# Last norm by rows, squares shared by two engines, a finer weave for one S5 group and for the first key steps

## What is computed

```
x <- LN0(a*x + 0.5*SwiGLU_1(x));  x <- LN1(a*x + Mix(x));  x <- LN2(a*x + 0.5*SwiGLU_2(x))
LN(x) = (x - mean) * rsqrt(mean((x - mean)^2) + 1e-5) * gain + bias        over the 1024 features
```

## Time and profile before

| | us |
|---|---|
| median of 3 runs (2525.97 to 2529.35) | 2529.04 |
| the profiled execution, its own time | 2529.85 |
| its span in the trace | 2528.2 |
| PE busy / DVE / ACT / POOL | 2406.3 / 1628.0 / 1086.1 / 458.9 |
| mean granted clock of PE, as a share of full | 0.982 |

### The profile page before, as it was taken

How to read it: one execution, slowest core, us unless ns; L and a number is a source line. 1 busy time by engine, 2 the same in 40 slices (tenths; PEclk the granted TensorE clock), 3 DMA queues, 4 the chain that set the end, 5 groups by cost and what they waited for, 6 DMA issues and landing times.

```text
span 2528.2 us, 46326 instructions
## 1 busy us (share of the span) xinstructions
PE 2406.3 (95%) x18811; PEld 2268.4 (90%) x18811; DVE 1628.0 (64%) x2536; ACT 1086.1 (43%) x1663; POOL 458.9 (18%) x532
## 2 busy tenths in 40 slices
PE   7999999999998999999999999999999889999998
PEld 6988998999787777789999999999999889999997
DVE  4787776665764555567686566466656585587555
ACT  3433455433553333443254534554433537354333
POOL 4896800002100111200111101021001000121000
PEclk9999999999999999999899999999999999999999
DMA  8667776445346777644566556555555556555553
GB/s 179 176 177 190 205 198 192 125 117 143 116 136 207 221 239 226 164 123 128 142 175 175 164 148 208 169 153 150 154 149 148 169 165 215 156 158 146 150 150 96
DMA packets 676278, 417.31 MB, mean 165 GB/s; under 512 B 31555, under 2 KB 639683, under 8 KB 676067
## 3 DMA queue, kind: packets, MB, share of 16 engines
q1 hardware_dynamic: 669538, 393.98, 54.1%
q0 software_dynamic: 6528, 20.37, 2.5%
HBM read 395.51 MB, written 18.78 MB: 164 GB/s over the span
## 4 chain that ended last, share of the span: by engine, by line
PE 78%; DVE 12%; issue 3%; ACT 3%; DMA 2%; SPq 2%; POOL 0%; POOLq 0%; ACTq 0%; DVEq 0%
PE ps L256 21%; PE ps L257 20%; PE ps L258 20%; DVE w_lo L251 4%; PE ps L881 2%; PE ps L882 2%; PE ps L883 2%; ACT w_hi L242 2%; PE ps L2280 1%; PE ps L1593 1%; PE ps L1642 1%; DMA w_raw<-in_ffn_w_up 1%; DVE x L531 1%; PE ps L1614 1%; DVE h_lo L435 1%
## 5 line engine op out<-in xcount | busy, mean ns | idle before, releaser
L251 DVE TENSOR_TENSOR w_lo<-w_raw,w_hi 128x1024 fp32r<-128x1024 f32 (+1 forms) x648 | 825.0, 1278 | 623.9 <-ACT w_hi L242 620.9
L256 PE MATMUL ps<-x_hi,w_hi 128*128 128x256 f32 (+1 forms) x3200 | 969.3, 303 | 49.4 <-DVE w_lo L251 35.9
L257 PE MATMUL ps<-x_lo,w_hi 128*128 128x256 f32 (+1 forms) x3200 | 955.9, 299 | 0.0
L258 PE MATMUL ps<-x_hi,w_lo 128*128 128x256 f32 (+1 forms) x3200 | 955.5, 299 | 0.0
L242 ACT ACTIVATE w_hi<-w_raw 128x1024 fp32r<-128x1024 f32 (+1 forms) x648 | 669.6, 1035 | 553.8 <-PE ps L258 399.5
L256 PEld LDWEIGHTS ps<-x_hi,w_hi 128*128 128x128 f32 x3200 | 616.2, 193 | 68.4 <-DVE w_lo L251 53.6
L257 PEld LDWEIGHTS ps<-x_lo,w_hi 128*128 128x128 f32 x3200 | 616.7, 193 | 1.1 <-issue 0.2
L258 PEld LDWEIGHTS ps<-x_hi,w_lo 128*128 128x128 f32 x3200 | 616.1, 193 | 0.0
L256 PE MATMUL ps<-h_hi,w_hi 128*128 128x256 f32 (+1 forms) x1408 | 423.9, 301 | 12.3 <-DVE w_lo L251 9.5
L257 PE MATMUL ps<-h_lo,w_hi 128*128 128x256 f32 (+1 forms) x1408 | 414.5, 294 | 0.0
L258 PE MATMUL ps<-h_hi,w_lo 128*128 128x256 f32 (+1 forms) x1408 | 414.4, 294 | 0.0
(11 more groups left out here) (263 smaller groups left out, 2192.8 us busy)
## 6 DMA issues: line engine op xcount, KB each, us to landing
w_raw<-in_ffn_w_gate SPq DMA_DIRECT2D x176, 512.0 KB, 4.2
w_raw<-in_ffn_w_up SPq DMA_DIRECT2D x176, 512.0 KB, 3.9
w_raw<-in_ffn_w_down SPq DMA_DIRECT2D x128, 512.0 KB, 4.0
w_raw<-in_w_in_ab SPq DMA_DIRECT2D x56, 512.0 KB, 4.0
w_raw<-in_ffn_w_down SPq DMA_DIRECT2D x64, 384.0 KB, 3.5
arena<-in_cache_k SPq DMA_DIRECT2D x64, 256.0 KB, 4.2
arena<-in_cache_v POOLq DMA_DIRECT2D x64, 256.0 KB, 4.8
w_raw<-in_w_out_ab SPq DMA_DIRECT2D x16, 512.0 KB, 3.9
```

Of the source, the lines that this page charges most:

```text
L251: dve.tensor_tensor(T.w_lo[:, u % RING, 0:n], T.w_raw[:, u % RAW, 0:n], T.w_hi[:, u % RING, 0:n].bitcast(F32), ALU.subtract).then_inc(T.w_ ...
L256: pe.matmul(out, w_hi, m_hi, start=first, stop=False)
L257: pe.matmul(out, w_hi, m_lo, start=False, stop=False)
L258: return pe.matmul(out, w_lo, m_hi, start=False, stop=last)
```

## The change

- `LastNorm` takes the place of N5B. DVE makes eight diagonal matrices of the gain during the last FFN, and SP loads the bias along rows. At the end PE multiplies the centred x by a diagonal, which turns it to rows and scales it by the gain (`to_rows`, 12 matmuls for each half of the features); ACT squares all eight blocks into eight buffers; PE sums the squares to one column for each token (24 matmuls with one moving column); ACT takes the root of 128x2 and 64x1 values and DVE inverts them; six DVE instructions multiply by the inverse root, add the bias and write the rows. Reciprocal, scaling and bias over 128x320 fall away, and the six copies and the 24 transposes.
- N0B, N2B and N3B are `shared`: POOL adds the squares of blocks 0 to 3 only, DVE adds those of 4 to 7 in step 3, and PE sums both, with two matmuls.
- In `f3a[:2]` the FFN yields after each product (`fine`), so that a side step follows each product and not each pair. `beside_b` takes the norm, the 11 input steps and the 14 scan steps singly, with six empty places between scan steps (`stretched`), and the outputs in pairs.
- `slowly` takes steps 0 to 4 singly, then (5, 6) and (7, 8) as pairs, so that all later steps come two main steps later.

```diff
-def ffn_tensor(T, pe, Q):
+def ffn_tensor(T, pe, Q, fine):
...
                     .then_inc(T.w_used.h, 1)
+                if fine and s == 0:
+                    yield
...
-            if i == self.var_at and self.alone:
-                for k in range(KT):
-                    pe.wait_ge(T.squared.h, self.squared + k + 1)
-                    pe.matmul(self.root_of, T.ones[:, :], T.sq[:, k % 4, 0:self.g.n], start=(k == 0), stop=(k == KT - 1))\
-                      .then_inc(T.sq_added.h, 1)
+            if i == self.var_at and self.shared is not None:
+                pe.wait_ge(T.sq_added.h, self.sq_added + 3)
+                pe.wait_ge(T.sq_shared.h, self.shared + 3)
+                pe.matmul(self.ps, T.ones[:, :], self.acc2, start=True, stop=False)
+                pe.matmul(self.ps, T.ones[:, :], self.acc, start=False, stop=True).then_inc(T.var_done.h, 1)
...
+            if i == self.square_at + 2 and self.shared is not None:
+                for k in range(5, KT):
+                    dve.wait_ge(T.squared.h, self.squared + k + 1)
+                    if k > 5:
+                        dve.wait_ge(T.sq_shared.h, self.shared + k - 5)
+                    dve.tensor_tensor(self.acc, T.sq[:, 0, 0:self.g.n] if k == 5 else self.acc, T.sq[:, k % 4, 0:self.g.n],
+                                      ALU.add).then_inc(T.sq_shared.h, 1)
...
+class LastNorm(Norm):
...
+    def tensor(self, pe, moved):
+        T = self.T
+        pe.wait_ge(T.acc_added.h, self.added + KT - 1)
...
+        pe.matmul(self.ps, T.ones[:, :], self.acc, start=True, stop=True).then_inc(T.sum_done.h, 1)
+        pe.wait_ge(T.const_ready.h, 4 + KT)
+        self.to_rows(pe, 0)
+        for k in range(KT):
+            pe.wait_ge(T.squared.h, self.squared + k + 1)
+            for i, t in enumerate(self.g.tiles):
+                m = P if t < PT else NS
+                mm = pe.matmul(self.var_ps[0:m, i:i + 1], self.sq[:, k, i * P:i * P + m], T.ones[:, 0:1],
+                               start=(k == 0 and i == 0), stop=(k == KT - 1), skip_group_check=True)
+        mm.then_inc(T.var_done.h, 1)
+        self.to_rows(pe, 1)
+
+    def to_rows(self, pe, q):
+        T = self.T
+        for k in range(4 * q, 4 * q + 4):
+            pe.wait_ge(T.centred.h, self.centred + k + 1)
+            for n, (t, of, m) in enumerate(self.places):
+                if of == q:
+                    mm = pe.matmul(T.ps[0:m, self.bank(n), (k % 4) * P:(k % 4 + 1) * P], T.x[:, k, t * P:t * P + m],
+                                   self.diag[:, k, :], start=True, stop=True)
+        mm.then_inc(T.y_turned.h, 1)
...
+    def vector(self, dve, rows, turned):
...
+        T.dve_chain(dve, dve.reciprocal(self.by_row[:, 0:2], self.by_row[:, 0:2]))
+        T.dve_chain(dve, dve.reciprocal(self.by_row[0:NS, 2:3], self.by_row[0:NS, 2:3]))
...
+            dve.scalar_tensor_tensor(rows[0:m, t, cols], T.ps[0:m, self.bank(n), :], self.by_row[0:m, i:i + 1],
+                                     self.bias_rows[0:m, cols], ALU.mult, ALU.add).then_inc(T.y_moved[0].h, 1)
...
-            return paced(steps, [s for s in range(AttendSamples.STEPS) if s >= 8 and s % 8 < 4])
+            return paced(steps, [s for s in range(AttendSamples.STEPS) if s < 5 or s >= 8 and s % 8 < 4])
...
-            first = Norm.STEPS - 2
-            return paced(norm_and_s5(norm, s5), range(first, first + S5Group.INPUTS))
+            scan = Norm.STEPS - 2 + S5Group.INPUTS
+            return stretched(paced(norm_and_s5(norm, s5), range(scan + S5Group.SCAN)), range(scan, scan + 12, 2))
```

More of the change, by code:

```diff
@@ L129, in paired, with spaced, stretched @@
     yield
+def spaced(steps):
+    for _ in steps:
+        yield
+        yield
+def stretched(steps, long):
+    for i, _ in enumerate(steps):
+        yield
+        if i in long:
+            yield
 def paced(steps, alone):
@@ L451, in ffn_gpsimd @@
             Q.norm.add(pool, d, Q.res)
+        if fine and d is None:
+            yield
         yield
@@ L461, with __init__ @@
     STEPS = 9
-    def __init__(self, T, g, row, scale, products, alone=False, slack=0):
-        self.alone, self.steps, n = alone, self.STEPS + 3 * slack, slack
+    def __init__(self, T, g, row, scale, products, slack=0, shared=False):
+        self.shared = T.sq_shared.take(3) if shared else None
+        self.steps, n = self.STEPS + 3 * slack, slack
         self.square_at, self.var_at, self.root_at = 1 + n, 4 + n, 4 + 2 * n
@@ L477, in __init__ @@
         self.sq_added, self.var, self.rooted, self.normed = (
-            c.take(k) for c, k in ((T.sq_added, KT if alone else KT - 1), (T.var_done, 1), (T.rstd_ready, 2), (T.normed, KT)))
+            c.take(k) for c, k in ((T.sq_added, 3 if shared else KT - 1), (T.var_done, 1), (T.rstd_ready, 2), (T.normed, KT)))
         self.affine, self.rounded, self.ready = (
@@ L572, in gpsimd @@
         for i in range(self.steps):
-            if i in (self.square_at, self.square_at + 1) and not self.alone:
+            if i in (self.square_at, self.square_at + 1):
                 for k in self.half(i, self.square_at):
-                    if k == 0:
+                    if k == 0 or k >= 4 and self.shared is not None:
                         continue
@@ L2771, in layers, with ffn @@
         F3B = Ffn(B, ffn_3, N4B.ready, N4B.affine + KT)
-        N5B = Norm(T, B, 5, 2.0, False, alone=True)
+        N5B = LastNorm(T, M, B, 5, 2.0, TT * D_MODEL)
         f3b = parts(F3B, (0, 1, 2), N5B)
-        before = {A: 0, B: 2 * len(A.tiles)}
-        whole = {A: N5A.affine + KT, B: N5B.affine + KT}
+        turned_a = 2 * len(A.tiles)
         y_rows = cut(0, TT, D_MODEL)
         block = ctx.enter_context(nc.Block())
-        def ffn(of, eng, parts):
+        def ffn(of, eng, parts, fine=False):
             for part in parts:
-                yield from of(T, eng, part)
-        def store_columns(pe, g):
-            yield from store_tensor(T, pe, g, before[g], whole[g])
+                yield from of(T, eng, part, fine)
         def norm_and_s5(norm, s5):
@@ L2835, in _ @@
             run(ffn(ffn_sync, sp, f2b))
-            weave(ffn(ffn_sync, sp, f3a[:2]), beside_b(idle(Norm.STEPS), s5_b.sync(sp, O)))
+            weave(ffn(ffn_sync, sp, f3a[:2], True), beside_b(idle(Norm.STEPS), s5_b.sync(sp, O)))
             run(out_sync(T, sp, OB2))
+            sp.wait_ge(T.res_done.h, OB2.res + KT)
+            N5B.load(sp, I["ln_b"][DEPTH - 1, 2])
             run(ffn(ffn_sync, sp, f3a[2:]))
@@ L2913, in _ @@
             weave(ffn(ffn_vector, dve, f2b), N4A.vector(dve))
-            weave(ffn(ffn_vector, dve, f3a[:2]), beside_b(N3B.vector(dve), s5_b.vector(dve)))
+            weave(ffn(ffn_vector, dve, f3a[:2], True), beside_b(N3B.vector(dve), s5_b.vector(dve)))
             run(out_vector(T, dve, OB2))
             weave(ffn(ffn_vector, dve, f3a[2:]), N4B.vector(dve))
-            weave(ffn(ffn_vector, dve, f3b), after(N5A.vector(dve), store_vector(T, dve, A, y_rows, before[A])))
-            run(after(N5B.vector(dve), store_vector(T, dve, B, y_rows, before[B])))
+            weave(ffn(ffn_vector, dve, f3b), after(after(N5A.vector(dve), store_vector(T, dve, A, y_rows, 0)),
+                                                    N5B.diagonals(dve)))
+            N5B.vector(dve, y_rows, turned_a)
         @block.gpsimd
@@ L2943, in _ @@
             weave(ffn(ffn_gpsimd, pool, f2b), N4A.gpsimd(pool))
-            weave(ffn(ffn_gpsimd, pool, f3a[:2]), beside_b(N3B.gpsimd(pool), s5_b.gpsimd(pool)))
+            weave(ffn(ffn_gpsimd, pool, f3a[:2], True), beside_b(N3B.gpsimd(pool), s5_b.gpsimd(pool)))
             run(out_gpsimd(T, pool, OB2))
```

96 lines of the change are left out of this document (72 added, 24 removed).

## The result

The changed kernel takes 2536.23 us (median of 8 runs, 2529.37 to 2541.2), the kernel before 2528.85 beside it (8 runs, 2525.97 to 2532.47). The ratio is 1.0027, with a 95% interval of 1.0018 to 1.0035: 6.8 us slower by the ratio, where 13.4 faster was forecast. The profiled run of the changed kernel is the fastest of its eight, 2529.37 us with a span of 2527.7. Since it is 6.9 us under its own median, a second trace of the same kernel was taken later (e15, span 2536.4), and both are read here.

The account below looks back on a forecast made before the run. PE was taken as the bound (busy 2406.3 of 2528.2 us), leaving its idle and low-clock time. Terms -3.2 + 0.5 - 3.7 - 7.0 = -13.4 from 2529.85 gave 2516.4, stated as 2516; 8-in-10 range 2505 to 2529.

Parts of the forecast that it names:

- the likeliest case: Whole kernel: the forecast itself, 13.4 us less, 2516 us, own range 2509 to 2523; chance 0.56.
- The third rival: Whole kernel: slower end and fine weave with more long waits, each costing 3.4 us at low clock; 2537 us; chance 0.10.
- one-column matmuls may leave the clock low, and the end is 2.2 slower: Last norm, clause of the third rival: one-column sums may keep the clock low, end 2.2 us slower.
- three new places in S5: Group B's S5, clause of the third rival: new waits over 3 us at three places, S5 6.5 us slower.
- The end, -3.2 forecast: From the last product: row products, one-column sums and six DVE instructions replace the old chain; 3.2 us less.
- 2.2 more: Upper bound of the end's term: 2.2 us more if the clock is low throughout.
- Shared norms, +0.5 forecast: N0B and N2B: DVE's adds finish earlier, but PE pays one more matmul; 0.5 us more, bounds 1 less, 2 more.
- Group B's S5, -3.7 forecast: N3B and S5: 1.8 us more at norm and transposes, scan 6.6 less, 1.1 given back; 3.7 us less.
- 18.5 lost: Group B's scan before the change: 58.8 us for 14 products worth 40.3 us, so 18.5 us lost.
- Key steps, -7.0 forecast: First key steps: single steps shorten PE's waits and avoid a clock fall; 7.0 us less, bounds 3 and 9.
- step 2 waits for keys that land at 795.6: Key step 2: PE arrives at 793.7 and waits 1.8 us for keys, instead of 3.60.
- Later steps shift by two main steps, in which nothing else is scarce: Later key steps: moving them two main steps later was taken to meet no other shortage.

Follow-up runs that it names:

- e15: The changed kernel run once more, nothing altered, for a second trace; 2537.2 us, ratio 1.0036 to the kernel before.
- e1: The kernel before with the new last norm (LastNorm) alone; 2532.97 us, ratio 1.0021.
- e4: The kernel before with the first key steps taken singly, alone; 2530.59 us, ratio 1.0010.
- e6: e4 with SP's list issuing the key pages of a sample step one step earlier; 2528.78 us, ratio 1.0003 to the kernel before.
- e2: The kernel before with the shared squares of N0B, N2B and N3B alone; 2527.29 us, ratio 0.9995.
- e3: The kernel before with the finer weave of group B's S5 alone; 2528.88 us, ratio 1.0000.
- e7: The kernel before, key steps still in pairs, with the whole sample list two main steps later on all engines; 2530.31 us, ratio 1.0010.
- e12: e11 plus single first key steps, key pages issued earlier and two later pairs put back together; 2518.78 us, ratio 0.9959 to the kernel before.
- e14: The whole change with its end mended as in e5; 2528.98 us, ratio 0.9999 to the kernel before.
- e5: The kernel before with LastNorm, but DVE adds the squares and PE does three one-column matmuls instead of 24; 2524.23 us, ratio 0.9984.
- e9: e1 with its 48 one-column passes placed behind both halves of the row products; 2532.31 us, ratio 1.0025 to the kernel before.
- e11: e5 with the shared norms added, old weave and old key steps; 2522.35 us, ratio 0.9974 to the kernel before.

## Why the prediction was wrong

The mechanism named for the likeliest case was wrong in sign, and the time was outside the range. The third rival, given 0.10, has 2537 for the whole, and its clause "one-column matmuls may leave the clock low, and the end is 2.2 slower" is what happened, only larger; its other clause, three new places in S5, is not. PE's waits of over 3 us around S5 went from one to three (3.40, 3.73 and 4.58), but the low clock of that stretch is 13.7 and 17.1 us after and 17.1 before, and the stretch is shorter. So that the time came out near this rival's 2537 is in part luck.

- **The end, -3.2 forecast.** e1 gives +5.3, the first trace +2.9, and like with like the ends give +5.4 and +7.4. Up to the sum of squares the steps hold in the first trace: `to_rows(0)` was over 5.5 us after the start of L778 (6.4 forecast; 8.1 in the second). The step that failed is the sum of squares and the clock behind it. 48 instructions were put at 4.6 us, by L1294's 0.115 and half of that; at full clock 16 take 2.00, so 48 take 5.9, and at the low clock 9.99 (9.2 was the bound given). The forecast had the clock low at first and full from 2513 on, as in the kernel before. But a level read in one trace is not a property of the place: three of the nine traces with the old end have it the other way. And the 48 passes brought the clock down, or kept it down, to the end of PE's work. `to_rows(1)` was then 7.16 us for 2.6, and DVE waited for it. 2.6 was too low in itself: 4.06 at full clock. The row meant to price it, the 24 transposes of L686, had the clock low for 3.3 of its 4.44 us and not for half; with a low clock throughout they take 5.38 us (e4, e6), and `to_rows` 7.16: the same shape is not the same price.

  With the clock full throughout the end would be 1.48 + 4.06 + 5.9 + 4.06 + 2.06 + 2.8 = 20.4 us, about the 19.9 forecast: two errors of size (+1.3 and +1.5), mostly offset by the 1.0 that `to_rows(0)` gained at full clock and by slack, and 5.6 to 9.6 us that are the clock's. The bound was "2.2 more" with the clock low throughout; e15, low from 2.1 us on, is 6.9 more (30.0). The prediction's own low prices, 5.1, 9.2 and again 5.1 for `to_rows(1)`, would have given 2.9 more. The rest is that each was too small: 6.6, 10.0 and 7.2 us.

  Root, reciprocals and scaling were right: 0.9 us for 1.0, 2.06 for three of 0.66.

  The Trainium skill, "TensorE: Matmul & The Clock Gate", section "LDWEIGHTS (loading the stationary operand)", gave 4.3 us for the 48 loads, an estimate; a group of six passes took 0.74 us at full clock, so 48 take 5.9. The page's figure is the load's own, and here it held as a lower bound only.
- **Shared norms, +0.5 forecast.** e2 gives -1.3 (-3.5 to +1.0). The wait in N0B fell from 3.43 to 3.22 (2.9 forecast), and the ruler has N0B's stretch 1.2 us shorter by the means. The miss is in N3B: without the fine weave PE's wait for the sum goes from 2.77 to 0.38 us, that for ACT from 1.94 to 0.69, and the stretch is 2.8 us shorter. The prediction priced N3B only together with the fine weave, where the wait is 3.40 (3.1 forecast), and so never saw that the norm alone was the gain.
- **Group B's S5, -3.7 forecast.** The waits were read rightly one by one: 3.40, 1.44 and 3.73 us (3.1, 1.6, 4.3), and in the scan 1.12, 1.59, 4.58 and 2.37 with small ones, 10.7 in all (11.2). Yet the fine weave alone is worth 0. What failed is the comparison, "18.5 lost" before against 11.9 after: the first holds whatever PE lost, low clock as well as waits (its idle time there was 13.1 us), and the second holds waits alone. Of the 6.6 us less, 2.4 are idle time saved in the changed kernel (13.1 to 10.7). In e3 the scan saves 3.2, but 2.3 come back at the norm and the transposes and 0.7 behind the scan, so that PE's idle time from piece 490 to 548 is 20.6 us for 20.8, with the clock low for 20.5 us and not 17.1. The stretch as a whole did become 1.8 to 3.6 us shorter in the changed kernel (3.7 forecast): that number came near by luck, for it is the shared norm's gain.
- **Key steps, -7.0 forecast.** e4 gives +2.5, the whole's stretch 407.7 and 411.2 for 408.5 (eight traces with the old pairs). Two steps failed. "step 2 waits for keys that land at 795.6" takes a DMA's time from the trace of before although the change moves its issue in SP's list; SP's list was not stepped through in the prediction as DVE's was. And "Later steps shift by two main steps, in which nothing else is scarce": e7 shows that this shift alone brings a wait of 3.18 us for a value page. With the first mended (e6) the stretch is 405.7 in its one trace, 2.8 us less than before, of which 1.7 may be the clock (low for 13.7 us, and for 17.1 in each of the eight); by its median e6 is no faster than the kernel before. That the singles help at all is not shown, and if they do it is by less than half of what was forecast.
- **What stood.** DVE is full through the scan, as forecast (busy 50.84 of 54.00 us from 2038 on), the softmax wait of 3.95 stays (3.94), and the eight diagonals cost nothing that is seen (from piece 548 to the last mean matmul all kernels agree within 0.03 us).

One thing stays open: what decides whether the clock falls within 3 us of the last mean matmul or holds. It does in nine of the seventeen traces (six old ends, e12, e14, e15) and not in eight (three old ends, after, e1, e5, e9, e11), with old and new code in both lots, and all come after the same idle of PE ahead of that matmul, 1.5 us. And the traces of every kernel but the changed one are single.

## What to carry to other kernels

Work that replaces long matmuls by many short ones must be priced at both levels of the clock, and what stands behind it too. A granted clock read in one trace is one draw, and no property of the place: take several, and compare ends that had the same level. If a matmul sums chunks that could be added first, let an idle engine do it: seven adds of up to 0.58 us on VectorE beside PE replaced 42 instructions and made the end 8.7 to 11.0 us shorter. When a list is stretched, walk every in-order queue again, and ask what its last steps, not its first, now lie beside. And take a change apart before it is judged: it was 6.8 us slower as a whole, and with two of its parts mended and one left out 10.4 faster.

## What the chip showed that was not expected

- A PE without a pause was at the lower clock for 13.5 us (after) and 23.0 us (e15), and in e14, with row products and only six one-column instructions, for 14.3. A chain of 48 one-column float32 instructions saw the clock fall in three of three traces in which it was full when they began, after 1.7 to 2.1 us.
- The same code at the same place had an early fall of the clock in six traces and none in three, and its end took 22.6 or 20.6 us.
- A float32 matmul instruction of 128 columns took 0.167 us at full clock and 0.298 at half, and a one-column one 0.123 and 0.207: more than half of the first is paid with one column, and half the clock costs less than twice the time.
